# The swap of a rotated projection tile moves behind the first attention part of the next tile

## The reference, cut to what matters

```python
def even_mixer(h, cos, sin, w_in, fgate_b, lq1, lk1, lq2, lk2, subln, w_out, layer_idx):
    aq, ak, av, af, bq, bk, bv = split_cols(h @ w_in, EVEN_SPLITS)
    ...
    q1 = apply_partial_rope(bq[..., 0, :], cs, sn)
    q2 = apply_partial_rope(bq[..., 1, :], cs, sn)
    k1 = apply_partial_rope(bk[..., 0, :], cs, sn)
    k2 = apply_partial_rope(bk[..., 1, :], cs, sn)
    ...
    o_b = diff_attention(q1, q2, k1, k2, bv.reshape(b, s, DIFF_HEADS, DIFF_V_DIM), lam)
    ...

def apply_partial_rope(x, cos, sin):
    half = ROT_DIM // 2
    xr = x[..., :ROT_DIM].astype(jnp.float32)
    x1, x2 = xr[..., :half], xr[..., half:]
    rot = jnp.concatenate([x1 * cos - x2 * sin, x2 * cos + x1 * sin], axis=-1)
    return jnp.concatenate([rot.astype(x.dtype), x[..., ROT_DIM:]], axis=-1)
```

## Time and profile before

| | |
|---|---|
| median of 3 runs | 2458.31 us (2449.61 to 2460.06) |
| the profiled execution | 2458.13 us |
| its span | 2456.3 us |
| TensorE busy in the span | 2295.8 us, 93% |
| VectorE, ScalarE, GpSimd busy | 1343.2, 865.8, 792.4 us |
| mean granted TensorE clock | 0.96 of full speed |

### The profile page before, as it was taken

How to read it: one execution, slowest core, us unless ns; L and a number is a source line. 1 busy time by engine, 2 the same in 40 slices (tenths; PEclk the granted TensorE clock), 3 DMA queues, 4 the chain that set the end, 5 groups by cost and what they waited for, 6 DMA issues and landing times. The chain is left out here.

```text
span 2456.3 us, 32514 instructions
## 1 busy us (share of the span) xinstructions
PE 2295.8 (93%) x11689; PEld 1855.8 (76%) x11689; DVE 1343.2 (55%) x2258; ACT 865.8 (35%) x1355; POOL 792.4 (32%) x378
## 2 busy tenths in 40 slices
PE   5999998889999999998999999999898799999998
PEld 4777997678878888775776788877676557888876
DVE  4487643487721774154456577721497662677601
ACT  3415111443322333233434333322324563433322
POOL 2000000424443444432213344444464004444442
PEclk8999986889999999999999999999999999999999
DMA  3320000323332233321212233333332003233232
GB/s 118 95 78 1 1 1 6 87 60 94 94 103 86 85 102 102 88 72 43 78 53 69 81 99 97 90 91 94 78 89 57 1 1 95 77 102 93 85 100 81
DMA packets 346541, 179.78 MB, mean 73 GB/s; under 512 B 16840, under 2 KB 343619, under 8 KB 346443
## 3 DMA queue, kind: packets, MB, share of 16 engines
q1 hardware_dynamic: 344842, 177.36, 25.2%
q10 hardware_dynamic: 1056, 1.06, 0.1%
q0 software_dynamic: 544, 0.06, 0.0%
HBM read 176.33 MB, written 2.13 MB: 73 GB/s over the span
## 5 line engine op out<-in xcount | busy, mean ns | idle before, releaser
L298 POOL TENSOR_TENSOR wlo<-raw,whi 128x1024 fp32r<-128x1024 f32 (+3 forms) x327 | 744.2, 2280 | 1585.8 <-ACT whi L294 925.8
L311 PE MATMUL banks<-xhi,whi 128*128 128x512 f32 x1536 | 611.5, 398 | 5.1 <-DVE cb L1038 3.9
L312 PE MATMUL banks<-xlo,whi 128*128 128x512 f32 x1536 | 602.8, 392 | 0.0
L313 PE MATMUL banks<-xhi,wlo 128*128 128x512 f32 x1536 | 602.6, 392 | 0.0
L311 PEld LDWEIGHTS banks<-xhi,whi 128*128 128x128 f32 x1536 | 291.5, 190 | 72.9 <-issue 9.1
L312 PEld LDWEIGHTS banks<-xlo,whi 128*128 128x128 f32 x1536 | 291.2, 190 | 63.4 <-issue 3.8
L313 PEld LDWEIGHTS banks<-xhi,wlo 128*128 128x128 f32 x1536 | 290.9, 189 | 61.1
L879 ACT ACTIVATE whi<-raw 128x1024 fp32r<-128x1024 f32 (+1 forms) x216 | 209.7, 981 | 191.3 <-DMA raw<-in_ffn_w_out_dram 87.7
L967 ACT ACTIVATE cb<-banks,conv 128x512 f32<-128x512 f32 x152 | 117.9, 778 | 445.9 <-DVE banks L1027 445.9
L311 PE MATMUL banks<-ghi,whi 128*128 128x512 f32 x608 | 239.7, 394 | 19.7 <-DVE xT L1069 13.8
L312 PE MATMUL banks<-glo,whi 128*128 128x512 f32 x608 | 238.2, 392 | 0.0
(11 more groups left out here) (453 smaller groups left out, 3081.9 us busy)
## 6 DMA issues: line engine op xcount, KB each, us to landing
raw<-in_ffn_w_in_dram SPq DMA_DIRECT2D x88, 512.0 KB, 3.9
raw<-in_w_ffn_up_dram SPq DMA_DIRECT2D x64, 512.0 KB, 4.1
raw<-in_w_ffn_down_dram SPq DMA_DIRECT2D x32, 512.0 KB, 4.3
raw<-in_ev_w_in_dram SPq DMA_DIRECT2D x25, 512.0 KB, 4.0
raw<-in_ffn_w_out_dram SPq DMA_DIRECT2D x32, 384.0 KB, 3.7
raw<-in_ffn_w_out_dram SPq DMA_DIRECT2D x32, 320.0 KB, 3.3
raw<-in_od_w_in_dram SPq DMA_DIRECT2D x20, 512.0 KB, 3.9
raw<-in_w_in_dram SPq DMA_DIRECT2D x19, 512.0 KB, 3.9
```

Source lines behind the costliest of these rows:

```text
L298: return pool.tensor_tensor(wlo[c][:, 0:n, :], raw[b][:, 0:n, :], whi[c][:, 0:n, :].bitcast(F32), ALU.subtract)
L311: pe.matmul(acc, whi[b][:, k, :], hi(k), start=first and k == 0, stop=False)
L312: pe.matmul(acc, whi[b][:, k, :], lo(k), start=False, stop=False)
L313: mm = pe.matmul(acc, wlo[b][:, k, :], hi(k), start=False, stop=last and k == n - 1)
```

## The change

The swap of tile `m - 1` was issued ahead of tile `m` for `m` from 9 to 12, and in its middle ahead of the attention part for `m` of 7 and 8. Now it is always issued in the middle and behind `units(m, 0)`. On VectorE the take of tile `m - 1` for `m` from 9 to 12 goes behind that step's first attention part, too.

```diff
                     if m >= lead.TILES:
-                        if m - 1 in ROT[2:] and m > DIFF:
-                            swap(m - 1)
                         pe.wait_ge(w_lo.h, s0 + m + 1)
                         if m >= 6:
                             pe.wait_ge(free.h, 1 if m == 6 else 2 if m == 7 else m - 1)
                         dense(m, 0, KD // 2)
                         if m in (4, 5):
                             swap(m - 4)
-                        if m - 1 in ROT[2:] and m <= DIFF:
+                        units(m, 0)
+                        if m - 1 in ROT[2:]:
                             swap(m - 1)
-                        units(m, 0)
...
                 for m in range(N):
-                    if m >= 1:
+                    if m >= 1 and not (m > DIFF and m - 1 in ROT):
                         take(m - 1)
...
                     units(m, 0)
+                    if m > DIFF and m - 1 in ROT:
+                        take(m - 1)
                     units(m, 1)
```

## The result

| | before | after |
|---|---|---|
| median | 2450.64 us (6 runs, 2442.07 to 2460.06) | 2434.68 us (6 runs, 2433.88 to 2443.43) |
| profiled execution, span | 2458.13 us, 2456.3 us | 2433.96 us, 2432.2 us |
| TensorE busy | 2295.8 us | 2280.1 us |
| mean granted clock | 0.960 | 0.967 |

The ratio is 0.9927 (95% interval 0.9901 to 0.9953): 0.7% faster, where 0.64% was forecast. Two further series with the changed kernel gave 0.9926 (0.9894 to 0.9959) and 0.9922 (0.9895 to 0.9950).

A forecast was written before the change was run, and what follows sets the result against it. TensorE was taken as the bound. Four stretches of 30.05 us, less 10.84 for clean ones and 3.6 for the swaps, gave 15.6 us (10.1 idle, 5.5 clock): 2458.1 - 15.6 = 2442.5 us, 0.64% less; range 2435 to 2452.

The forecast's parts named there:

- The base: Whole kernel: the profiled execution's 2458.13 us, from which the gain of 15.6 us was subtracted to give 2442.5 us.
- The idle time, 10.1 us: TensorE's four stops at the swaps of tiles 8 to 11, waiting for ScalarE's copy, would go: 10.1 us gained.
- The clock's share, 5.5 us: Slow TensorE clock behind those stops would go: 5.5 us of the gain; the windows' mean clocks gave 5.0 us.
- The swap's own price, 0.9 us: Each of the four moved swaps still pushes TensorE's next matmuls back 0.9 us; together 3.6 us, bounds 3.4 to 4.4.
- The copy is there in time: At the swap's new mid-tile place, TensorE arrives 1.0 us after tile 9's copy ends, at least 0.4 us; no wait.
- VectorE has 1.2 us to spare: With the take moved, VectorE reaches the second attention part 1.2 us before TensorE finishes its scores; price nothing.
- The clock did not fall by itself: Rival: TensorE still runs parts of these tiles at 1.2 GHz, so only 10.1 us are gained, 2448.0 us; chance 0.1.
- no wait stood in the middle of a tile: Rival: the copy is late at the swap's new place; 4 or 8 us stay, 2446.5 or 2450.5 us; chance 0.1.
- the flip's wait: Rival: a later wait, like the flip's 2.9 us for VectorE, absorbs all of the gain, 2458 us; chance 0.05.
- the ring: Rival: swap, take, reduction, exponentials, copy, next swap (5.7 us) set the pace; slower, 2470 us; chance 0.03.
- The signs: Profile after: no swap waits, clock 1.00 from 1100 to 1190, steps 9.3 to 10.1 us, busy 5 and span 15 lower.

The follow-up runs named there:

- VectorE's half: Kernel before, with only VectorE's take moved behind the first attention part while TensorE still swaps ahead of the tile; 2443.23 us in a single execution.
- filled stops: Kernel before, with 12 matmuls (7 for tile 10) added ahead of each swap of tiles 8 to 11 to fill TensorE's idle time; 2445.16 us, single execution.
- smaller split: Changed kernel, with GpSimd splitting only one block of eight of weight tiles 10 to 18 of the stage; 2430.24 us, single execution.

## Why the prediction was wrong in its range, and where it was right

**The base.** The step that failed is the sum's starting point, "2458.1 - 15.6 = 2442.5 us", and with it the range that was hung on it. I took one profiled execution and its three neighbours as the kernel's time. All six runs give 2450.64 us, and 2450.64 - 15.6 = 2435.0, 0.4 us from what was measured. The runs of before in all series together lie in three groups, 4 at 2438.8 to 2442.1, 20 at 2446.2 to 2453.0 and 16 at 2458.1 to 2462.3 us. Those of the changed kernel do the same some 16 us lower: 5 at 2423.1 to 2429.4, 10 at 2433.9 to 2435.6, 8 at 2441.4 to 2445.8. The profiled execution of before belonged to the upper group, that of after to the middle one. The term was 7.5 us too high (2458.1 against 2450.6), and that is nearly all of the 7.8 us between 2442.5 and 2434.68. That the time fell just outside and not just inside is chance: over all series the medians are 2450.86 us (40 runs) and 2435.15 (23 runs), 15.7 us apart, and 2435.15 lies in the range. The table shows most of what sets the groups apart:

| profile | clock, 360 to 450 us | tile 8 reached, us | time, us |
|---|---|---|---|
| before, first | 0.69 | 1104.66 | 2458.13 |
| before, second | 0.81 | 1096.17 | 2449.48 |
| VectorE's half | 0.90 | 1089.86 | 2443.23 |
| changed, first | 0.81 | 1095.07 | 2433.96 |
| changed, second | 0.67 | 1105.05 | 2445.79 |
| changed, third | 0.68 | 1106.61 | 2441.43 |

The same kernel is found at either level, so this is no effect of the change. It is not all: the third profile of the changed kernel reached tile 8 1.6 us later than the second and ended 4.4 us earlier. From tile 13 to 1230 us its mean clock was 1.00 and that of the second 0.96, from 1860 to 1990 us 0.92 and 0.89. Why an execution falls on one or the other stays open. The range hung on the same step: it saw the spread of the three runs (it names 2434 for one such as the lowest) and then began at 2435 all the same; it should have begun lower.

**The idle time, 10.1 us.** Right: the stops at the swap went from 10.09 us to none, and moving VectorE alone left all four as they were.

**The clock's share, 5.5 us.** Right against the first profile, as the window's 15.6 us say, and too large as a constant: the second profile of the same kernel has 1.7 us less of it behind the same stops, and the filled stops put it at 3.2 to 4.9 us. The 5.5 was what the sum had left over, and held 0.6 us more than the clock took even in the first profile (4.9); the 5.0 that the windows' clocks gave was nearer. Where the 0.6 went isn't shown. By the windows of the two profiles the change is worth 13.8 to 15.6 us.

**The swap's own price, 0.9 us.** Right: steps with a swap are 9.61 and 10.06 us, the clean ones of the same shape 8.74 and 9.16, a difference of 0.87 and 0.90.

**The copy is there in time.** Right: the copy of tile 9 ended at 1112.20 and its swap began at 1113.33, 1.1 us later, 1.0 predicted.

```profile
1111.62 0.58 ACT L2103 ACTIVATE bk<-banks 128x512 f32<-128x512 f32 x1
```

**VectorE has 1.2 us to spare.** Right in the step of tile 9 (1.1 us), wrong in those of tiles 10 and 12. There a product was stretched to 2.5 us, the take ended 6.0 us behind the start of the part, and VectorE began the next scores at 1117.99, when TensorE had ended them at 1117.73: 0.3 us late instead of early. It cost nothing: TensorE shows no wait there, as the flips need the normalizing only later. The whole margin that I argued with was gone, and that I had not seen.

**The rivals.** The clock did not fall by itself (1.00 over 46 us), no wait stood in the middle of a tile, the flip's wait stayed at 2.87 us and took nothing, and the ring did not set the pace: the copies of tiles 8 to 11 ended 1.1 to 3.1 us ahead of their swaps.

**The signs.** Three came out other than named. From 1100 to 1190 us the clock was 0.98 and not 1.00, since the low clock behind the flip's stop, which the kernel before has at 1200 us, now falls into that window. The step from tile 9 to tile 10 took 9.17 us, under the 9.3 to 10.1. And busy time and span fell by 15.7 and 24.1 us instead of 5 and 15, by what came from ahead of tile 8.

## What to carry to other kernels

A wait of the bounding engine for an answer that is on its way is removed by putting work that doesn't need the answer ahead of it in the same queue; read from the trace when the answer is ready and when the queue would get there, and check the same for each engine whose order follows. Count with the stop what the clock takes behind it, but as a range. And before a small gain is subtracted from a time, look whether the runs shown fall into groups: the size of the gain is taken from the stage, the base from all runs.

## What the runs showed of the hardware that I had not expected

**GpSimd's split stretches VectorE's products in SBUF.** GpSimd and VectorE in the changed kernel:

```profile
1113.22 2.38 POOL L298 TENSOR_TENSOR wlo<-raw,whi 128x1024 fp32r<-128x1024 f32 x1 [4.07 <-ACT whi L294]
...
1169.09 3.40 POOL L298 TENSOR_TENSOR wlo<-raw,whi 128x1024 fp32r<-128x1024 f32 x1 [4.97 <-ACT whi L294]
```

```profile
1113.37 2.52 DVE L1193 TENSOR_SCALAR ex<-ex,mx 128x512 f32<-128x512 f32 x1
1115.92 0.75 DVE L1194 SCALAR_TENSOR_TENSOR ex<-ex,mx 128x512 f32<-128x512 f32 x1
...
1161.90 2.50 DVE L1194 SCALAR_TENSOR_TENSOR ex<-ex,mx 128x256 f32<-128x256 f32 x1
...
1169.09 1.21 DVE L2218 TENSOR_TENSOR_SCAN ak<-ak 8x512 f32<-8x512 f32 x1
1170.33 2.44 DVE L2219 TENSOR_SCALAR ak<-ak 8x512 f32<-8x512 f32 x1
```

A product of 0.5 us that begins while the split of 2.38 us runs ends with it (1115.89 against 1115.60), for one tensor with a scalar (line 1193) and for two tensors (line 1194). Products that read a PSUM bank in such a time aren't stretched: the reductions at 1103.88 beside a split from 1103.48 took 0.56 and 0.55 us, as at 1117.69 in the kernel before, where no split ran. The Trainium skill, "GPSIMD Engine Reference", section "1. Specifications", says that GpSimd shares its way to SBUF with VectorE and that two kinds of VectorE instructions contend for it, those in a mode with two ports and those with two inputs in SBUF. The trace agrees for the two inputs in SBUF. For the product of one tensor it agrees in that it is stretched, but no row names the mode; where nothing ran beside them, line 1193 took 0.51 ns more for each further column (0.28 us for 128, 0.41 for 384) and line 1194 1.05 (0.35 and 0.62).

It goes the other way as well. The split at 1169.09 begins with VectorE's scan of 1.21 us and takes 3.40 us, 1.0 more than the others; with the smaller split the same pair has this:

```profile
1170.19 1.47 POOL L298 TENSOR_TENSOR wlo<-raw,whi 128x128 fp32r<-128x128 f32 x1 [6.91 <-ACT whi L294]
```

The other splits of that size took 0.45 to 0.47 us.

In the kernel before, the splits of tiles 8 to 12 ran while VectorE waited or did its take, which reads a PSUM bank, so that its rows didn't show it in these tiles: taking a stop away also moved two engines' work onto each other. Later in the stage the kernel before had it too, ahead of the flip:

```profile
1194.58 2.44 DVE L2219 TENSOR_SCALAR ak<-ak 8x512 f32<-8x512 f32 x1
```

**A stop of the same length may or may not be followed by a low clock.** The stop of 2.58 us behind tile 8 was followed by a swap of 1.94 us and a stretch at 0.69 in the first profile. In the second profile of the same kernel, and with VectorE's half alone, the same stop had no low clock behind it (the first row is of the former, the others of the latter):

```profile
1102.79 1.10 PE L1985 MATMUL banks<-bq,sw 128*128 128x512 f32 x2 [2.57 <-ACT bq L2105]
```

```profile
1096.48 1.10 PE L1985 MATMUL banks<-bq,sw 128*128 128x512 f32 x2 [2.58 <-ACT bq L2105]
...
1108.83 2.05 PE L1985 MATMUL banks<-bk,sw 128*128 128x512 f32 x2 [2.94 <-ACT bk L2105]
```

The stops of 2.94 us were followed by one in all three of these profiles, the flip's of 2.87 us in two of the changed kernel's three. No stop of 1.63 us or less in these tiles was followed by one in any profile. Which it will be for a stop of 2.6 to 2.9 us isn't shown; that is why the clock's share is given as a range.
